# Weight tiles 4 to 48 and 53 to 76 loaded from ScalarE's DMA queue instead of SyncE's

## What is computed

```
p = rmsnorm(h, norm_mix) @ w_in            # qkv_a, z_a, a, b, q_b, k_b, v_b, gate_a, gate_b
o_a = gated delta rule over qkv_a (causal conv, chunks of the prompt; one step for the samples)
o_b = stick-breaking attention with q_b, k_b, v_b
      (prompt: causal; each sample also reads 16 pages of 128 keys and values from cache_k, cache_v)
m = sigmoid(gate_a) * (o_a @ w_pa) + sigmoid(gate_b) * (o_b @ w_pb)
h = h + m @ w_o
h = h + (silu(g) * up) @ w_ffn_out,  g, up = split(rmsnorm(h, norm_ffn) @ w_ffn_in)
y = rmsnorm(h, norm_final)
```

## Time and profile before

| what | value |
|---|---|
| median of three runs | 1377.97 us |
| the profiled execution | 1375.76 us, its span 1373.8 us, the other 2.0 us lie around it |
| TensorE (PE) busy | 1320.0 us, 96% of the span |
| VectorE (DVE) busy | 796.5 us, 58% |
| ScalarE (ACT) busy | 527.3 us, 38% |
| DMA, SyncE's queue | 262.75 MB |
| DMA, ScalarE's queue | 1.06 MB |

### The profile page before, as it was taken

The page is one execution under the profiler, slowest core; times in us unless marked ns, Lnnn a source line. Parts: engine busy times, 40 slices in busy tenths (PEclk is TensorE's granted clock), DMA queues, the critical chain, the costliest instruction groups (busy, mean ns, idle before and its releaser), DMA issues.

```text
span 1373.8 us, 27805 instructions
## 1 busy us (share of the span) xinstructions
PE 1320.0 (96%) x10527; PEld 1215.4 (88%) x10527; DVE 796.5 (58%) x2973; ACT 527.3 (38%) x797; POOL 179.5 (13%) x252
## 2 busy tenths in 40 slices
PE   6999999998999899999999999999999999999998
PEld 5999977787798787878988788999999999999998
DVE  4689759958889857886564223345544444433222
ACT  4333366537865422334334332234422222222222
POOL 1000001005220352400310000000211111110000
PEclk9999999999999969998999999999999999999999
DMA  8559968767743288989789986423333333323232
GB/s 309 172 179 321 326 214 295 259 230 264 243 116 101 80 287 310 366 301 321 219 243 329 372 283 199 139 78 93 90 92 94 95 91 93 94 87 88 85 100 74
DMA packets 256859, 265.56 MB, mean 193 GB/s; under 512 B 22987, under 2 KB 215677, under 8 KB 255927
## 3 DMA queue, kind: packets, MB, share of 16 engines
q1 hardware_dynamic: 256295, 262.75, 59.1%
q10 hardware_dynamic: 432, 1.06, 0.2%
HBM read 244.26 MB, written 19.70 MB: 192 GB/s over the span
## 4 chain that ended last, share of the span: by engine, by line
PE 75%; DVE 7%; SPq 5%; DMA 4%; ACT 4%; issue 2%; POOL 1%; POOLq 0%; ACTq 0%; DVEq 0%
PE ps L1177 57%; PE ps L1289 3%; PE ps L1215 3%; PE ps L1300 1%; SPq L781 1%; DMA wring<-in_w_in 1%; SPq L847 1%; PE ps L1274 1%; DVE kring L2402 1%; DVE R L2483 1%; PE ps L1474 1%; SPq L923 1%; DVE wring_split L646 1%; DVE R L2521 1%; DVE vring L2524 1%
## 5 line engine op out<-in xcount | busy, mean ns | idle before, releaser
L1177 PE MATMUL ps<-obT_split,wring_split 128*128 128x268 f32 (+2 forms) x1296 | 263.5, 285 | 0.0
L1177 PE MATMUL ps<-obT_split,qv_split 128*128 128x260 f32 (+2 forms) x1024 | 213.9, 290 | 4.0 <-DVE wring_split L646 1.9
L646 DVE TENSOR_TENSOR wring_split<-wring,vring_split 128x1024 fp32r<-128x1024 f32 (+1 forms) x92 | 118.4, 1286 | 144.2 <-ACT vring_split L640 144.2
L1177 PEld LDWEIGHTS ps<-obT_split,wring_split 128*128 128x128 f32 (+1 forms) x1296 | 200.7, 188 | 0.5
L1177 PE MATMUL ps<-obT_split,vring_split 128*128 128x260 f32 (+1 forms) x960 | 195.8, 285 | 0.7 <-issue 0.7
L1177 PE MATMUL ps<-xn_split,vring_split 128*128 128x260 f32 (+1 forms) x960 | 193.2, 282 | 0.0
L1177 PE MATMUL ps<-xn_split,qv_split 128*128 128x260 f32 (+2 forms) x896 | 182.0, 285 | 0.0
L1177 PEld LDWEIGHTS ps<-obT_split,qv_split 128*128 128x128 f32 (+1 forms) x1024 | 157.6, 188 | 20.8 <-issue 16.1
L1177 PEld LDWEIGHTS ps<-obT_split,vring_split 128*128 128x128 f32 x960 | 147.7, 188 | 3.2 <-issue 2.9
L1177 PEld LDWEIGHTS ps<-xn_split,vring_split 128*128 128x128 f32 x960 | 148.0, 188 | 0.1
L640 ACT ACTIVATE vring_split<-wring 128x1024 fp32r<-128x1024 f32 (+1 forms) x92 | 95.0, 1034 | 136.8 <-DMA wring<-in_w_ffn_out 84.2
(11 more groups left out here) (424 smaller groups left out, 2114.0 us busy)
## 6 DMA issues: line engine op xcount, KB each, us to landing
wring<-in_w_in SPq DMA_DIRECT2D x72, 512.0 KB, 6.3
kring<-in_cache_k SPq DMA_DIRECT2D x64, 512.0 KB, 5.5
wring<-in_w_ffn_in SPq DMA_DIRECT2D x44, 512.0 KB, 3.7
vring<-in_cache_v SPq DMA_DIRECT2D x32, 512.0 KB, 5.6
kring<-in_cache_v SPq DMA_DIRECT2D x32, 512.0 KB, 5.8
vring<-in_cache_k SPq DMA_DIRECT2D x24, 512.0 KB, 5.7
R<-in_cache_k SPq DMA_DIRECT2D x24, 512.0 KB, 6.6
obT<-in_cache_v SPq DMA_DIRECT2D x24, 512.0 KB, 6.7
```

What stands on the lines that cost most here:

```text
L646: nc.vector.tensor_tensor(fr(w_part(wlo[:, p % RING, :], p)), w_part(wring[:, p % RING, :], p), w_part(w_high(p), p), ALU.subtract).then_i ...
L1177: last = mm(ps[0:m, tile_bank(t) + i, 0:n], fr(w), fr(x[k][:, a + i * n:a + i * n + n]), start=(k == 0 and w is w_h and x is hi), stop=(k ...
```

## The change

The loads of tiles 4 to 48 and 53 to 76, 69 in all, are taken out of SyncE's stream and issued by ScalarE, each right behind its read of tile p - 4. Tiles 0 to 3, 49 to 52, and those from 77 on stay with SyncE. Each load keeps its wait for TensorE. The semaphores of the key stores are divided in another way (one for each half of the columns), and ScalarE waits for the stores of the first half at value tile 20 and for the second at tile 21, where it waited for both at tile 21.

```diff
+T_PA = T_SEG + 8 * KT
...
-            for p in range(RING, T_SEG + 3):
-                w_load(sp, p)
...
-                      .then_inc(k_out[t % 2], 16)
+                      .then_inc(k_out[half], 16)
...
-                    if t != 2 * KT and T_SEG + t + 3 < T_Z or s >= 5 and T_SEG + t + 3 < T_O:
+                    if T_SEG + t + 3 == T_Z + 3 or T_SEG + t + 3 >= T_PA + RING:
                         w_load(sp, T_SEG + t + 3)
...
-                    w_load(sp, T_SEG + 2 * KT + 3)
...
+            def next_load(t):
+
+                if t + RING < T_Z or T_Z <= t < T_PA:
+                    w_load(act, t + RING)
+
             def read_tile(t, dst, func=ACT.Copy, m=P):
                 act.wait_ge(w_used, done(t))
                 go(halves(dst[:, first_token(t):TOKENS]), pair(t, m), func).then_inc(act_read, 1)
+                next_load(t)
...
+                        if (s, j) == (1, 3):
+                            act.wait_ge(k_out[0], 16 * 6)
                         if (s, j) == (1, 4):
-                            act.wait_ge(k_out[0], 16 * 8)
-                            act.wait_ge(k_out[1], 16 * 4)
+                            act.wait_ge(k_out[1], 16 * 6)
...
                         go(zsv[:, j, :], ps[:, b + 1, 252:260], ACT.Silu).then_inc(act_read, 1)
+                        next_load(t)
```

More of the change, by code:

```diff
@@ L623, in wait_read, with w_load @@
             eng.wait_ge(act_read if reader(t) == "act" else dve_read, READ_COUNT[t])
-        def w_load(sp, p):
+        def w_load(eng, p):
             name, col, k0, k1, n = pieces[p]
             if p >= RING:
-                sp.wait_ge(w_used, p - RING + 1)
+                eng.wait_ge(w_used, p - RING + 1)
             dst = wring[:, p % RING, :].rearrange("p (k n) -> p k n", k=KT)[:, 0:k1 - k0, 0:n]
             src = io[name][k0 * P:k1 * P, col:col + n].rearrange("(k p) n -> p k n", p=P)
-            sp.dma_start(dst, src).then_inc(w_in_slot[p % RING], 16)
+            eng.dma_start(dst, src).then_inc(w_in_slot[p % RING], 16)
         def split_hi(act, t):
@@ L856, in store_keys @@
                     sp.dma_start(io["k_prompt"][t * P:t * P + n, c:c + 512], ktok[0:n, t, c:c + 512])\
-                      .then_inc(k_out[t % 2], 16)
-                sp.dma_start(io["k_sample"][:, c:c + 512], ktok[LASTP:LAST, 4, c:c + 512]).then_inc(k_out[0], 16)
+                      .then_inc(k_out[half], 16)
+                sp.dma_start(io["k_sample"][:, c:c + 512], ktok[LASTP:LAST, 4, c:c + 512]).then_inc(k_out[half], 16)
             def store_values():
@@ L1099, in _ @@
             sp.wait_ge(y_out, 16 * 5)
-            sp.wait_ge(k_out[0], 16 * 8)
-            sp.wait_ge(k_out[1], 16 * 4)
+            sp.wait_ge(k_out[0], 16 * 6)
+            sp.wait_ge(k_out[1], 16 * 6)
             sp.wait_ge(v_out, 16 * 6)
```

## The result

| | before | changed |
|---|---|---|
| median of 20 runs | 1373.01 us (1369.00 to 1378.41) | 1378.93 us (1373.81 to 1386.06) |
| ratio | | 1.0042, 95% interval 1.0029 to 1.0056 |
| the profiled execution, its span | 1373.8 us | 1384.3 us |

The change makes the kernel slower by 0.42%, 5.8 us. More runs of the kernel before put its median at 1373.01, 5 us under that of the three which the prediction had; so a forecast of 1373.7 turns out to be "no change", and its direction, faster by 4.3, is wrong. The profiled execution after is among the slower ones (1386.04 us), that of before 1375.76; the two differ by 10 us, the kernels by 5.8.

A forecast was written before the change was run, and what follows sets the result against it. TensorE was taken to bound the kernel, busy 1320.0 of 1373.8 us. Terms of -0.49, -2.00, -0.5 and -1.3 summed to -4.3 us, giving 1373.7 against the median of 1377.97; range 1366 to 1381.

The forecast's parts named there:

- The ceiling: PE's gaps in q, key, value, convolution and gate tiles that a weight or SyncE's order can touch: 15.17 us.
- ScalarE's own cost: On ScalarE's queue, the 69 load instructions run beside its reads and cost nothing: 0.
- Rival D: On ScalarE's queue, loads hold ScalarE and what PE waits for behind them: +8.7 us, 1386.7; chance 0.13.
- The added wait: At value tile 20, ScalarE's earlier wait for the first half's stores costs nothing: 0.
- Term 1: In the q tiles, loads no longer stand behind SyncE's other work; the gap at 46.60 goes: -0.49 us.
- Term 2: In key and value tiles, weights 15 and 20 go out earlier; gaps of 0.90 and 1.10 go: -2.00 us.
- Term 3: In the convolution tiles, earlier weights remove the 3.15 gap but the wait mostly moves on: -0.5 us, between 0 and -9.44.
- Term 4: In the gate tiles, moved weight 61 fills a DMA hole and pages come earlier: -1.3 us, between 0 and -3.24.
- Rival C: In convolution and gate tiles, weights on another queue pass the pages, delaying quads: +0.7 us, 1378.7; chance 0.17.

The follow-up runs named there:

- none: No load moved, only the divided key-store semaphores and ScalarE's earlier wait, against the kernel before: ratio 0.9996 (0.9974 to 1.0018).
- start: Only tiles 4 to 28 (q, keys, values) loaded from ScalarE, against the kernel before: ratio 0.9971 (0.9953 to 0.9989).
- wide_sp: The kernel before with the 69 loads, still on SyncE, as 4 KB rows from other places of `w_in`: ratio 0.9936 (0.9919 to 0.9954).
- gate: Only tiles 53 to 76 (z, gates, w_pa) loaded from ScalarE, against the kernel before: ratio 1.0002 (0.9985 to 1.0019).
- burst_wide: Only tiles 29 to 32 loaded from ScalarE, as 4 KB rows from another place of `w_in`, against the kernel before: ratio 0.9991 (0.9974 to 1.0007).

## Why the prediction was wrong

*The ceiling* (15.17 us of idle time behind weights and pages) was read correctly, and three of the four terms had the right sign. The forecast's list held no term that could come out above zero. Its own mark was that PE's idle time falls by 2 to 7 us; it rose by 11.8.

*ScalarE's own cost, 0.* Right. Its loads took 0.37 to 0.43 us each, its busy time is 527.3 us before and after. Rival D, ScalarE held for microseconds, did not happen once.

*The added wait, 0.* Right as far as it can be measured: none is at 0.9996 (0.9974 to 1.0018).

*Term 1, -0.49.* Right: the gap at 46.60 is gone, the row comes at 45.86 in the first trace.

*Term 2, -2.00.* The gaps of 0.90 and 1.10 are gone (a small one of 0.29 and 0.56 stands at 122 to 123 in the two traces), and the sum of both terms, 2.49, was 2.03 and 1.19 in the two traces at the end of the value tiles; the timed start gave 4. But not for the reason given. Weight 15 was issued at 95.57, with the start of the read and not at its end (96.9) as worked out, and the rounding, which the prediction had in good time, still waited for it:

```profile
95.57 0.37 ACTq L633 DMA_DIRECT2D wring<-in_w_in  x1
...
112.44 1.06 ACT L641 ACTIVATE qv_split<-wring 128x1024 fp32r<-128x1024 f32 x1 [9.60 <-DMA wring<-in_w_in]
```

12.8 us of earlier issue bought 2.5 us (112.44 against 114.95 of the earlier trace rows), and 0.7 of these is the lead that PE and the read of tile 11 had already (95.56 against 96.29); PE needed 0.90.

*Term 3, -0.5, between 0 and -9.44.* **This step failed**, in its size and sign: it was +5.0 to the third quad's sums, and +7.6 and +6.8 in the two traces to the matmul at 360.06, with the granted clock at 0.50 for a part of it, which the sum had no term for. It held that the bytes ahead of the pages stay the same, and that a weight issued earlier arrives earlier. The bytes did stay the same. What changed is who waits for them. In SyncE's queue, before, a weight landed behind the pages issued ahead of it and ahead of those issued after it: the first quad, issued from 290.9 to 295.6, took 6.7 to 7.8 us to landing, and weights 29 and 30 followed at 304.6 and 306.5; weight 31, issued at 303.06, landed at 310.9, a key page issued at 304.26 at 312.2. On ScalarE's queue pages issued later landed first: two key pages issued at 295.99 and 297.8 were there at 307.6 and 309.1, weight 30, issued at 290.50, at 312.6, 22.1 us after its issue instead of 10.0. Weight 34 was issued at 331.47, 3.3 us earlier than before and not 6.6, because the tiles ahead of it were late. The upper end of 0 was argued from the share of 1.06, which says that the DMA engines are full and nothing about how two queues divide them. It should have been left open above, since no row of the trace had two queues busy at once with different packets: the three DMAs of the earlier trace rows on ScalarE's queue are of another kind.

*Term 4, -1.3.* The sign fits, the size is not shown: the two waits went from 3.24 to 1.68 and 1.64 in the two traces, and they are 1.57 to 2.17 in all five traces with gate tiles from ScalarE. But with the gate tiles on SyncE they are 1.8 to 3.4 in ten traces (start has 0.98 + 0.80) and nothing in wide_sp. A gain of this size is below what the timed gate kernel can show. Weights were starved here as well (weight 66 took 15.9 us to land), but were not needed so soon.

*Rival C* asked the right question, whether the queues are served side by side, and gave the wrong answer, that the weights would pass the pages. It was priced at +0.7 and its mark was a landing within 4 us; here the pages passed the weights. From 292 to 310 each queue moved 1700 packets. Read with the sizes of the packets this tells the sign: equal counts give a queue of 512-byte packets an eighth of what a queue of 4 KB packets gets, and measured were 0.86 MB beside 6.16. With the packets of 512 bytes the issuing engine made the difference between 7.8 to 10.0 us to landing (before) and, for the first three of the four weights, 17.0 to 22.1 (changed).

## What to carry to other kernels

Before a load is moved to another engine's queue, compare the packets of both queues, not only their bytes: beside a queue full of 4 KB packets, one of 512-byte packets got an eighth of the bytes here (0.86 of 7.02 MB from 292 to 310), and what is needed soonest should not be in it. Ask of each moved load what is queued elsewhere while it is under way: where pages come in bursts (four loads of 69 here), keep it in their queue, ahead of them. And read the greatest landing time beside the median: here the median fell from 6.3 to 5.7 us while three of the four loads that mattered doubled. A wait of PE cost more than its own length here: behind that of 5.84 us the granted clock was 0.50 until 356, and the 16 sums of a quad took 3.64 us instead of 1.92.

## What the runs showed of the hardware that was not expected

- Two DMA queues with work moved equal numbers of packets, of 3.6 and 0.5 KB in the mean: 1700 and 1700 in 18 us (1600 and 1600 in 17 us in the second trace), and with it 0.86 MB of 7.02 MB for the queue with 512-byte packets. With 4 KB packets on the same queue (burst_wide, 290 to 307) it got 1.39 MB of 6.42 MB, though it moved no packet from 303 to 305, when its first two loads had landed.
- A load on ScalarE's queue went out before the operation ahead of it had begun: that of tile 33 at 320.88, while the read in front of it started at 324.19.
- The 69 loads in packets of 4 KB, the same number of bytes on the same queue, made the kernel 8.8 us faster (wide_sp, 0.9936), though not by earlier landings in the stretch looked at (7.5 to 11.2 us against 7.8 to 10.0). That their source was only 8 blocks of `w_in` may have part in it.
- Behind PE's wait of 5.84 us, in a stretch in which it was mostly idle from 340 on (busy 2.18 of 7 us), the granted clock was 0.50 for all of 347 to 356, and the 16 sums of a quad took 3.64 us instead of 1.92.
